# Expert weights held still in the array: gate and up products with 32-column strips of the weights stationary and 88 tokens moving

## The chip, the cores and the metric

The kernel runs on one core of a Trainium2 chip. The metric is the device time of one execution in microseconds. Three runs of the kernel before gave 1382.76, 1383.42 and 1383.52 us, so 1383.42 us is the median.

## What is computed

A trunk of two layers works on 256 frames of width 1024, all in float32. The part that the change touches is the expert layer of layer 1: a router picks two of eight experts for each frame, and each expert is a SwiGLU of inner width 3584. Cut to what matters:

```python
def moe_swiglu(h, w_router, b_router, w_gu, w_down):
    logits = (h @ w_router).astype(jnp.float32) + b_router.astype(jnp.float32)
    top_logit, top_idx = lax.top_k(logits, TOP_K)              # TOP_K = 2 of N_EXPERTS = 8
    top_w = jax.nn.softmax(top_logit, axis=-1)
    gates = jnp.sum(jax.nn.one_hot(top_idx, N_EXPERTS) * top_w[..., None], axis=-2)
    out = jnp.zeros_like(h)
    for e in range(N_EXPERTS):
        out = out + gates[..., e:e + 1] * swiglu(h, w_gu[e], w_down[e])

def swiglu(h, w_gu, w_down):
    gate, up = jnp.split(h @ w_gu, 2, axis=-1)                 # w_gu[e]: 1024 x 7168
    return (jax.nn.silu(gate) * up) @ w_down                   # w_down[e]: 3584 x 1024
```

Everything else (the mixers, the dense feed-forward block, the norms, the gated embeddings) is the same in both kernels.

## The kernel before

**Items and units.** The expert layer is worked off in items. An item is one expert with at most CAP = 96 of its tokens; with these inputs the eight experts have 53 to 84 tokens, so eight items run. An item has EU = 7 units of 512 inner features, and a unit has six granules of 1 MB of weights: four for gate and up, two for down. The granules go through a ring of six slots of 1 MB (three in the tile raw, three in the tile SC), so the transfers can be one unit ahead. SyncE's queue loads each granule as two halves of 512 KB (L318 for gate and up, L385 for down); each half waits on the count `used`, which TensorE raises when it has read the half that lay there.

**Gate and up.** For each side (gate, up) and each k of 8 slices of the inputs, `strips` multiplies three groups of 32 tokens (stationary, 32 columns of the array each) with 512 weight columns (moving). The array's 128 columns are used as four strips of 32: three strips take 384 weight columns each (L970), the fourth takes the remaining 128 weight columns of the three groups one after the other (L968). So a side and k are six matmuls, and a unit has 16 such calls. A float32 matmul of the program is two weight loads and two passes in the trace, four TensorE instructions.

**Down.** The hidden values of a unit are multiplied by the two down granules in four rounds of nine matmuls (L1005 with 512 moving columns, L1009 and L1014 with 256), with 32 tokens stationary and weights moving. They accumulate over the item's units in two banks.

**Between the two.** ScalarE takes the SiLU of the gate bank (L1425), VectorE multiplies by the up bank (L2038), and then turns the product, since the down product needs features on partitions: 16 block transposes of 32x96 (L2047) from hh into he. TensorE does the gate and up products of unit u+1 before the down product of unit u, so these steps have a whole gate and up phase of time.

**Loops.** TensorE's program is straight code for the layers before, for the first unit and for item 0; then a loop over items 1 to 6 (L1099), then the last item. Each item is straight code for one unit (gate and up of unit 1, down of unit 0) followed by an inner loop over its remaining units (L1075), whose body is one unit. The body of the inner loop has 96 + 36 = 132 matmuls, that is 528 TensorE instructions and 5 more; the body of the loop over items, which holds the straight unit, the 12 small matmuls of `turn_rows` and the inner loop once, is 1,100 instructions.

Of the kernel before, what the change touches and what calls it, by code (L numbers as in the profile page):

```python
# [22 lines left out]
ALU = mybir.AluOpType  # L23
ACT = mybir.ActivationFunctionType
# [19 lines left out]
def trunk(nc, x_d, pT_d, columns_d, norm_g, w_in_ab, a_ln_g, a_ln_b, wsT_d, w_out_ab, ffn_w_gu,  # L44
# [11 lines left out]
    ITEM = 6 * EU  # L56
    CAP = 96
    MAIN = 4 * CAP
    XTRA = T * P * 2 // (CAP + 1)
# [16 lines left out]
    with ExitStack() as ctx:  # L76
# [117 lines left out]
        xe = gain[:, 0:KT * CAP].rearrange("p (k c) -> p k c", c=CAP)  # L194
        xg_turned = xn[:, 0, 0:KT * CAP].rearrange("p (k c) -> p k c", c=CAP)
        ye = raw[:, 0, 0:D]
# [62 lines left out]
        def raw_part(g, s):  # L259
            k = raw_slot(g)  # L260
            return raw[:, k, s * HW:(s + 1) * HW] if k < RAW else more_raw[k - RAW][:, s * HW:(s + 1) * HW]

        def raw_count(g, turns):
# [45 lines left out]
        def _(sp):  # L309
# [114 lines left out]
        def _(pool):  # L424
# [69 lines left out]
            pool.wait_ge(lg_done, 1)  # L494
            pool.memset(xg_rows[0:CAP, :], 0.0).then_inc(rows_clear, 1)
            pool.wait_ge(rows_zero, 16)
# [42 lines left out]
        def _(pe):  # L539
# [416 lines left out]
            def turn_rows():  # L956

                for t in range(T):
                    for a in range(2):
                        for c in range(0, CAP, 32):  # L960
                            m = pe.matmul(PS[c:c + 32, 3, 0:2], sel16[:, t, c:c + 32], pick[:, t, a, :],
                                          start=(t == 0 and a == 0), stop=(t == T - 1 and a == 1), skip_group_check=True)
                m.then_inc(rows_psum, 1)

            def strips(bank, tokens, w, start, stop):

                for k in range(CAP // 32):
                    pe.matmul(PS[CAP:P, bank, k * P:(k + 1) * P], tokens[k], w[:, MAIN:N], start=start and k == 0, stop=stop,  # L968
                              skip_group_check=True)
# [4 lines left out]
            def landed(g, s, turns):  # L974
                pe.wait_ge(raw_full[raw_slot(g)][s], raw_count(g, turns))

            def unit_gu(g, turns, sides=(0, 1), quarters=False):

                for side in sides:
                    for k in range(KT):  # L980
                        h, j = k // HK, k % HK
                        if quarters and j % 2 == 0:
                            pe.wait_ge((xg_act, xg_ready)[j // 2], h + 1)
                        granule = g + 2 * side + h
                        if j % 2 == 0:
                            landed(granule, j // 2, turns)
                        m = strips(side, [xe[:, k, c:c + 32] for c in range(0, CAP, 32)],
                                   raw_part(granule, j // 2)[:, j % 2 * N:(j % 2 + 1) * N], k == 0, k == KT - 1)
                        if j % 2:
                            m.then_inc(used, 1)  # L990

            def turned_tokens(b, block=he):
                if b < 3:
                    return [block[:, b * P + a:b * P + a + 32] for a in range(0, CAP, 32)]
                return [block[:, k * P + CAP:(k + 1) * P] for k in range(3)]

# [3 lines left out]
            def wide_round(g, j, r, start):  # L1000
# [11 lines left out]
                def rest(k):  # L1012
                    c = k % 2 * (N // 2)
                    return pe.matmul(PS[CAP:P, 4 + k // 2, c:c + N // 2], tokens[k], w[:, N + N // 2:2 * N],  # L1014
                                     start=start and k != 1, stop=True, skip_group_check=True)
# [11 lines left out]
            def unit_down(g, n, turns, first=False):  # L1027
                pe.wait_ge(hT_ready, n)
                for j in range(2):
                    for r in range(2):  # L1030
                        landed(g + j, r, turns)
                        m = wide_round(g, j, r, first and j == 0 and r == 0)
                        m.then_inc(used, 1)

            def unit_down_last(g, n, turns, first=False):
                pe.wait_ge(hT_ready, n)
                for j in range(2):
                    for r in range(2):
                        landed(g + j, r, turns)
                        for c in range(2):  # L1040
                            m = down_round(g, j, r, c, first and j == 0 and r == 0, True)
                        m.then_inc(used, 1)

            def last_down(g, n, turns):

                pe.wait_ge(hT_ready, n)
                for j, r, c in ((0, 0, 0), (0, 0, 1), (0, 1, 0), (0, 1, 1), (1, 0, 0), (1, 1, 0), (1, 0, 1), (1, 1, 1)):
                    if c == 0:
                        landed(g + j, r, turns)
                    m = down_round(g, j, r, c, False, j == 1 and r == 1, he_last)  # L1050
# [72 lines left out]
        def _(act):  # L1123
# [292 lines left out]
            def xg(n):  # L1416

                act.wait_ge(rows_turned, n)
                for k in range(HK):
                    m = act.activation(xe[:, k, :], xg_turned[:, k, :], ACT.Copy,  # L1420
                                       scale=vcol[:, V_N12 + k:V_N12 + k + 1])
                m.then_inc(go_act, 1)

            def unit_silu():
                act.activation(sg[:, 0:MAIN], PS[:, 0, 0:MAIN], ACT.Silu).then_inc(silu_done, 1)  # L1425

# [8 lines left out]
            def output(g, turns):  # L1435

                product(g, turns)
                banks = PS[:, 4:6, :].rearrange("p b n -> p (b n)")
                act.activation(yo[0:CAP, 0:768], banks[0:CAP, 0:768], ACT.Copy)
                for k in range(3):  # L1440
                    m = act.activation(yo[32 * k:32 * (k + 1), 768:D], banks[CAP:P, 256 * k:256 * (k + 1)], ACT.Copy)
                m.then_inc(y_evac, 1)
# [43 lines left out]
            for c in range(2):  # L1486
                if c == 0:
                    act.wait_ge(y_half, Y_MOE + 1)
                else:
                    product(G_MOE, ended)  # L1490
                act.activation(ye[0:CAP, c * N:c * N + MAIN], PS[0:CAP, 4 + c, 0:MAIN], ACT.Copy).then_inc(ye_act, 1)

# [21 lines left out]
        def _(dve):  # L1514
# [501 lines left out]
            def turn_xg(n):  # L2016

                dve.wait_ge(x_rows, n * 16)
                for to in range(0, P, 32):
                    for of in range(0, CAP, 32):  # L2020
                        m = dve.transpose(xg_turned[to:to + 32, :, of:of + 32],
# [3 lines left out]
            def xg(n):  # L2025
                dve.wait_ge(rows_turned, n)
                for k in range(HK, KT):
                    m = dve.tensor_scalar(xe[:, k, :], xg_turned[:, k, :], vcol[:, V_N12 + k:V_N12 + k + 1], None,
                                          ALU.mult)
# [5 lines left out]
            def unit_hidden(n):  # L2035
                dve.wait_ge(silu_done, n)
                dve.wait_ge(hT_ready, n - 1)
                dve.tensor_tensor(hh[:, 0:MAIN], sg[:, 0:MAIN], PS[:, 1, 0:MAIN], ALU.mult).then_inc(h_ready, 1)  # L2038
# [132 lines left out]
            def last_turn(i):  # L2171

                unit_turn(i * EU + (FB + 1), (i * EU - 1) * (2 * RING) + 2 * (G_MOE + 10))

            dve.wait_ge(used, 2 * (G_MOE + 4))
            unit_hidden(FB + 1)
# [13 lines left out]
            for c in range(2):  # L2190
# [4 lines left out]
                for k in range(3):  # L2195
                    m = dve.tensor_copy(ye[32 * k:32 * (k + 1), c * N + MAIN:(c + 1) * N], PS[CAP:P, 4 + c, k * P:(k + 1) * P])
                m.then_inc(ye_rest, 1)
# [83 lines left out]
```

## Time and profile before

| | before |
|---|---|
| median of three runs | 1383.42 us |
| the profiled execution | 1383.38 us |
| its span, first to last instruction | 1381.6 us |
| outside the span | 1.8 us |
| TensorE busy | 1369.5 us (99%) |
| TensorE weight loads busy | 1180.4 us (85%) |
| VectorE busy | 675.7 us (49%) |
| ScalarE busy | 311.1 us (23%) |
| granted TensorE clock | 1.000 |

The span runs from the first to the last instruction on the chip; the time of a run is 1.8 us longer. Weight loads overlap the matmuls. Matmuls of different strips run at the same time, so the duration of one is not its share of the time: what counts is the distance of starts in one strip. The expert layer lies between about 460 and 1336 us. "issue" in a view is time in which an engine waited for nothing that the profile shows. Queue q8 of the DMA engines carries instructions, q1 the weights, q0 the gathers and scatters of token rows.

### The profile page before, as it was taken

What the parts mean: (1) busy time and instruction counts of PE and PEld (TensorE: products, weight loads), DVE (VectorE), ACT (ScalarE), POOL (GpSimd) and SP (SyncE); (2) the same over time, 40 slices, a digit from 0 to 9 for tenths busy, and PEclk for the clock granted to TensorE, in tenths of its full rate; (3) what the DMA queues carried; (4) which work ended last, traced back from release to release, by engine and by line L of the source; (5) the groups of instructions that cost most, each with busy time, mean ns of one, the idle gap of its engine ahead of it and who ended that gap; (6) DMA issues with size and microseconds to landing.
All of it is one profiled execution on the core that took longest, in us unless ns stands there. A gap on an engine that the chain in (4) does not pass through costs nothing.

```text
span 1381.6 us, 43318 instructions
## 1 busy us (share of the span) xinstructions
PE 1369.5 (99%) x18176; PEld 1180.4 (85%) x18179; DVE 675.7 (49%) x1677; ACT 311.1 (23%) x514; POOL 40.0 (3%) x61
## 2 busy tenths in 40 slices
PE   8999999999999999999999999999999999999998
PEld 6888888888788888898888888888888888889986
DVE  7886555556886533522433432532433342254454
ACT  7465444446543200100000000000000010011112
POOL 1010000000000000000000000000000000000000
PEclk9999999999999999999999999999999999999999
DMA  8477555547424999999999999999999999999970
GB/s 322 174 247 246 191 189 186 191 168 244 154 93 162 385 390 410 409 401 409 408 401 409 407 402 408 407 398 410 408 398 410 406 409 397 409 396 409 409 283 31
DMA packets 123591, 448.60 MB, mean 325 GB/s; under 512 B 14476, under 2 KB 14476, under 8 KB 122896
## 3 DMA queue, kind: packets, MB, share of 16 engines
q1 hardware_dynamic: 119232, 435.21, 82.0%
q0 software_dynamic: 4160, 12.58, 2.7%
q8 instruction: 39, 0.64, 0.2%
q14 instruction: 16, 0.13, 0.0%
q10 hardware_dynamic: 144, 0.03, 0.0%
HBM read 442.71 MB, written 7.34 MB: 326 GB/s over the span
## 4 chain that ended last, share of the span: by engine, by line
PE 98%; DVE 1%; issue 0%; ACT 0%; POOL 0%; POOLq 0%; DVEq 0%; ACTq 0%
PE PS L970 43%; PE PS L541 10%; PE PS L543 10%; PE PS L542 10%; PE PS L1005 9%; PE PS L1014 9%; PE PS L968 2%; PE PS L592 1%; PE PS L1009 1%; PE PS L836 0%; PE PS L682 0%; PE PS L610 0%; DVE he_last L2047 0%; PE PS L1103 0%; PE PS L946 0%; PE PS L926 0%
## 5 line engine op out<-in xcount | busy, mean ns | idle before, releaser
L2047 DVE STREAM_TRANSPOSE he<-junk 32x96 f32<-32x96 f32 x880 | 237.5, 270 | 212.2 <-PE PS L1005 180.4
L970 PE MATMUL PS<-raw,gain 128*32 128x384 f32 x2712 | 328.1, 491 | 0.0
L970 PE MATMUL PS<-SC,gain 128*32 128x384 f32 x2664 | 323.3, 491 | 0.0
L968 PE MATMUL PS<-raw,gain 128*32 128x128 f32 x2712 | 305.6, 273 | 0.0
L968 PE MATMUL PS<-SC,gain 128*32 128x128 f32 x2664 | 299.8, 273 | 0.0
L968 PEld LDWEIGHTS PS<-SC,gain 128*32 128x32 f32 x2664 | 290.9, 110 | 8.2
L968 PEld LDWEIGHTS PS<-raw,gain 128*32 128x32 f32 x2712 | 295.3, 110 | 0.2
L541 PE MATMUL PS<-w_hi,xT_hi 128*128 128x512 f32 x536 | 212.9, 397 | 2.8 <-DVE w_lo L1532 1.6
L543 PE MATMUL PS<-w_lo,xT_hi 128*128 128x512 f32 x536 | 209.0, 390 | 0.0
L542 PE MATMUL PS<-w_hi,xT_lo 128*128 128x512 f32 x536 | 208.7, 389 | 0.0
L1425 ACT ACTIVATE junk<-PS 128x384 f32<-128x384 f32 x56 | 27.7, 495 | 763.8 <-PE PS L970 763.8
L970 PEld LDWEIGHTS PS<-SC,gain 128*32 128x32 f32 x2664 | 190.2, 108 | 0.2
L970 PEld LDWEIGHTS PS<-raw,gain 128*32 128x32 f32 x2712 | 185.4, 108 | 0.0
L2038 DVE TENSOR_TENSOR junk<-junk,PS 128x384 f32<-128x384 f32 x56 | 31.0, 554 | 307.4 <-ACT junk L1425 297.9
L1532 DVE TENSOR_TENSOR w_lo<-raw,w_hi 128x1024 fp32r<-128x1024 f32 x144 | 168.8, 1220 | 22.1 <-ACT w_hi L1131 20.4
L1005 PE MATMUL PS<-raw,he 128*32 128x512 f32 x588 | 154.9, 593 | 0.0
L1005 PE MATMUL PS<-SC,he 128*32 128x512 f32 x588 | 154.5, 592 | 0.0
L1131 ACT ACTIVATE w_hi<-raw 128x1024 fp32r<-128x1024 f32 x144 | 145.4, 1064 | 26.9 <-PE PS L543 15.2
L1014 PE MATMUL PS<-raw,he 128*32 128x256 f32 x588 | 134.9, 379 | 0.0
L1014 PE MATMUL PS<-SC,he 128*32 128x256 f32 x588 | 134.9, 379 | 0.0
L1009 PE MATMUL PS<-raw,he 128*32 128x256 f32 x588 | 123.1, 379 | 0.0
L1009 PE MATMUL PS<-SC,he 128*32 128x256 f32 x588 | 123.1, 379 | 0.0
(312 smaller groups left out, 1512.0 us busy)
## 6 DMA issues: line engine op xcount, KB each, us to landing
raw<-in_e_w_gu SPq DMA_DIRECT2D x226, 512.0 KB, 8.5
SC<-in_e_w_gu SPq DMA_DIRECT2D x222, 512.0 KB, 8.5
SC<-in_e_w_down SPq DMA_DIRECT2D x114, 512.0 KB, 8.5
raw<-in_e_w_down SPq DMA_DIRECT2D x110, 512.0 KB, 8.5
raw<-in_ffn_w_gu SPq DMA_DIRECT2D x44, 512.0 KB, 4.7
raw<-in_w_in_c SPq DMA_DIRECT2D x32, 512.0 KB, 5.3
raw<-in_ffn_w_down SPq DMA_DIRECT2D x22, 512.0 KB, 5.3
raw<-in_w_in_ab SPq DMA_DIRECT2D x20, 512.0 KB, 6.1
```

The costliest lines, as they stand in the source:

```text
L541: pe.matmul(out, a_hi, b_hi, start=start, stop=False, skip_group_check=True)
L542: pe.matmul(out, a_lo, b_hi, start=False, stop=False, skip_group_check=True)
L543: return pe.matmul(out, a_hi, b_lo, start=False, stop=stop, skip_group_check=True)
L968: pe.matmul(PS[CAP:P, bank, k * P:(k + 1) * P], tokens[k], w[:, MAIN:N], start=start and k == 0, stop=stop, skip_group_check=True)
L970: m = pe.matmul(PS[32 * k:32 * (k + 1), bank, 0:MAIN], tokens[k], w[:, 0:MAIN], start=start, stop=stop, skip_group_check=True)
L1005: return pe.matmul(PS[32 * k:32 * (k + 1), 4, :], tokens[k], w[:, 0:N], start=start, stop=True, skip_group_check=True)
L1009: return pe.matmul(PS[32 * k:32 * (k + 1), 5, 0:N // 2], tokens[k], w[:, N:N + N // 2], start=start, stop=True, skip_group_check=True)
L1014: return pe.matmul(PS[CAP:P, 4 + k // 2, c:c + N // 2], tokens[k], w[:, N + N // 2:2 * N], start=start and k != 1, stop=True, skip_group_c ...
L1131: act.activation(w_hi[:, g % RING, part], raw_part(g, s), ACT.Copy).then_inc(hi_done, 1)
L1532: dve.tensor_tensor(w_lo[:, g % RING, part], raw_part(g, s), w_hi[:, g % RING, part].bitcast(F32), ALU.subtract).then_inc(lo_done, 1)
L2038: dve.tensor_tensor(hh[:, 0:MAIN], sg[:, 0:MAIN], PS[:, 1, 0:MAIN], ALU.mult).then_inc(h_ready, 1)
L2047: m = dve.transpose(block[to:to + 32, :].rearrange("p (b c) -> p b c", c=P)[:, :, of:of + 32], hh[of:of + 32, 0:MAIN].rearrange("p (b c) - ...
```

## The change

Four things change together, all in the expert layer.

1. **Gate and up.** `feature_strips` takes the place of `strips` there: the weights are stationary, 32 columns at a time in each of the array's four strips, and the expert's 88 tokens move. A side and k are 16 matmuls instead of 6. A strip's 32 columns are taken with a stride of two floats. The result has features on partitions and tokens along the free dimension. CAP falls from 96 to 88; the layout of the down product stays at 96 (SLOTS).
2. **Transfers.** Each granule is one transfer of 1 MB, 8 KB for each partition, that waits until both halves of its slot are read; TensorE waits once for a granule.
3. **The turn.** Since the hidden values come out with features on partitions, the 16 transposes become one copy of 128x384 from hh to he (its wait on `used`, that is until the last down product has read he, stays).
4. **The program's size.** Gate and up have 256 matmuls in a unit instead of 96, so a unit has 292 matmuls: the inner loop's body is 1,173 TensorE instructions, where it was 533, and the body of the loop over items 2,379, where it was 1,100. The whole TensorE program is 14,526 instructions, where it was 10,048. An instruction is 64 bytes.

```diff
-    CAP = 96
-    MAIN = 4 * CAP
+    CAP = 88
+    SLOTS = 96
+    MAIN = 4 * SLOTS
...
+            def load_whole(g, src, turns, first=False):
+                back, free = (RAW, lo_done) if first else (RING, used)
+                sp.wait_ge(free, turns * 2 * RING + 2 * (g - back) + 2)
+                sp.dma_start(raw_whole(g), src).then_inc(raw_full[raw_slot(g)][0], 16)
...
-                    load(g + q, src.rearrange("e g p n -> p (e g n)"), turns, first and q < RAW)
+                    load_whole(g + q, src.rearrange("e g p n -> p (e g n)"), turns, first and q < RAW)
...
-                    for s in range(2):
-                        src = dn[bass.ds(e, 1), bass.ds(u * (N * D) + (2 * j + s) * P * D, P * D)]
-                        sp.wait_ge(used, turns * 2 * RING + (2 * (g + j - RING) + s + 1))
-                        sp.dma_start(raw_part(g + j, s), src.rearrange("e (p m) -> p (e m)", p=P)).then_inc(
-                            raw_full[raw_slot(g + j)][s], 16)
+                    src = dn[bass.ds(e, 1), bass.ds(u * (N * D) + 2 * j * P * D, 2 * P * D)]
+                    load_whole(g + j, src.rearrange("e (p m) -> p (e m)", p=P), turns)
...
+            def feature_strips(side, k, w):
+
+                paired = w.rearrange("p (j c r) -> p j r c", j=2, r=2)
+                for b in range(4):
+                    for f in range(4):
+                        m = pe.matmul(PS[32 * f:32 * (f + 1), side, b * SLOTS:b * SLOTS + CAP], paired[:, b // 2, b % 2, 32 * f:32 * (f + 1)],
+                                      xe[:, k, :], start=(k == 0 and b == 0), stop=(k == KT - 1), skip_group_check=True)
+                return m
...
-                        if j % 2 == 0:
-                            landed(granule, j // 2, turns)
-                        m = strips(side, [xe[:, k, c:c + 32] for c in range(0, CAP, 32)],
-                                   raw_part(granule, j // 2)[:, j % 2 * N:(j % 2 + 1) * N], k == 0, k == KT - 1)
+                        if j == 0:
+                            landed(granule, turns)
+                        m = feature_strips(side, k, raw_part(granule, j // 2)[:, j % 2 * N:(j % 2 + 1) * N])
...
-                for to in range(0, P, 32):
-                    for of in range(0, P, 32):
-                        m = dve.transpose(block[to:to + 32, :].rearrange("p (b c) -> p b c", c=P)[:, :, of:of + 32],
-                                          hh[of:of + 32, 0:MAIN].rearrange("p (b c) -> p b c", c=P)[:, :, to:to + 32])
-                m.then_inc(hT_ready, 1)
+                dve.tensor_copy(block[:, :], hh[:, 0:MAIN]).then_inc(hT_ready, 1)
```

On TensorE, at the head of the inner loop's body (raw_full4a and 4b are the arrivals of the two halves of ring slot 4; gain holds the expert's tokens xe), before:

```order
L1075 UNCONDITIONAL_BRANCH
L1078 REGISTER_ALU [waits go_dve,go_act]
L975 ISA [waits h_ready]
L968 MATMUL PS<-SC,gain 32x128 [waits raw_full4a]
L970 MATMUL PS<-SC,gain 32x384
L968 MATMUL PS<-SC,gain 32x128 [waits raw_full4b]
L970 MATMUL PS<-SC,gain 32x384
```

There a half granule is 12 matmuls, six of each form, of which the fence shows the first two. The same place of the change:

```order
L1091 UNCONDITIONAL_BRANCH
L1094 REGISTER_ALU [waits go_dve,go_act]
L985 ISA [waits h_ready]
L992 MATMUL PS<-gain,SC 32x88 [waits raw_full4a]
L992 MATMUL PS<-gain,SC 32x88 x63
L992 MATMUL PS<-gain,SC 32x88 [waits raw_full5a]
L992 MATMUL PS<-gain,SC 32x88 x63
```

A granule is now 64 matmuls behind one wait, where it was 24 behind two. On VectorE, in the inner loop, the product with the up bank and the turn of it, before:

```order
L2037 REGISTER_ALU [waits silu_done]
L2038 TENSOR_TENSOR junk<-junk,PS 128x384 [waits hT_ready]
L2044 ISA [waits h_ready]
L2047 STREAM_TRANSPOSE he<-junk 32x3x32 [waits used]
L2047 STREAM_TRANSPOSE he<-junk 32x3x32 x15
```

and with the change (junk is the tile that hh lies in):

```order
L2053 REGISTER_ALU [waits silu_done]
L2054 TENSOR_TENSOR junk<-junk,PS 128x4x88 [waits hT_ready]
L2061 ISA [waits h_ready]
L2062 COPY he<-junk 128x384 [waits used]
```

Sixteen instructions became one behind the same waits.

## Rows read from the trace of the kernel before

**Rows 1.** The page, busy time of each engine, instruction queue, and the chain by engine
```profile
PE 1369.5 (99%) x18176; PEld 1180.4 (85%) x18179; DVE 675.7 (49%) x1677; ACT 311.1 (23%) x514; POOL 40.0 (3%) x61
...
q8 instruction: 39, 0.64, 0.2%
...
PE 98%; DVE 1%; issue 0%; ACT 0%; POOL 0%; POOLq 0%; DVEq 0%; ACTq 0%
```
**Rows 2.** Waits of SyncE's queue, 600 to 1200: line, released by, total, times, longest
```profile
SPq L318 <- PE PS L970: 197.7, 307, 1.0
SPq L385 <- PE PS L1005: 103.0, 152, 0.7
```
**Rows 3.** The chain that ended last, 610 to 650: start, us, what
```profile
612.98 10.26 PE PS L970 x94
...
628.64 10.26 PE PS L970 x94
644.30 5.79 PE PS L970 x53
```
**Rows 4.** Windows: length, PE, PEld, DVE, ACT, POOL busy (x), clock, DMA, GB/s
```profile
628.16:643.82 15.66, 15.66 (x271) 13.47 (x265) 4.88 (x17) 0.50 (x1) 0.00 (x0) 1.00 1.03 409
683.55:793.44 109.89, 109.89 (x1867) 95.43 (x1862) 41.27 (x143) 6.46 (x15) 1.90 (x2) 1.00 1.03 406
460.00:1336.00 876.00, 875.77 (x14959) 773.39 (x14958) 345.92 (x1185) 66.24 (x136) 16.51 (x18) 1.00 1.02 405
448.00:452.00 4.00, 3.87 (x24) 2.32 (x23) 2.23 (x4) 1.98 (x5) 0.84 (x2) 1.00 1.02 424
```
**Rows 5.** Timeline of PE, 628.6 to 629.9: start, us, instruction
```profile
628.69 0.27 PE L968 MATMUL PS<-SC,gain 128*32 128x128 f32 x1
...
628.80 0.27 PE L968 MATMUL PS<-SC,gain 128*32 128x128 f32 x1
```
**Rows 6.** Groups of PE, PEld and DVE, 600 to 1200: busy, mean ns | idle
```profile
L968 PE MATMUL PS<-SC,gain 128*32 128x128 f32 x1847 | 208.0, 273 | 0.0
L1005 PE MATMUL PS<-SC,he 128*32 128x512 f32 x456 | 119.9, 592 | 0.0
L1014 PE MATMUL PS<-SC,he 128*32 128x256 f32 x456 | 104.6, 379 | 0.0
L968 PEld LDWEIGHTS PS<-SC,gain 128*32 128x32 f32 x1844 | 201.4, 110 | 6.5
L2047 DVE STREAM_TRANSPOSE he<-junk 32x96 f32<-32x96 f32 x615 | 166.0, 270 | 149.9 <-PE PS L1005 142.3
```
**Rows 7.** Timeline of PE, around 365 and 371
```profile
365.27 1.30 PE L815 MATMUL PS<-SC 128*32 128x32 f32 x128
...
370.83 0.77 PE L836 MATMUL PS<-SC 128*32 128x16 f32 x69
372.77 0.69 PE L836 MATMUL PS<-SC 128*32 128x16 f32 x59 [1.17 <-issue]
```
**Rows 8.** Windows of straight-line code, columns as in Rows 4
```profile
366.10:371.65 5.55, 5.50 (x143) 4.33 (x129) 4.79 (x5) 2.08 (x3) 0.00 (x0) 1.00 0.79 286
381.90:386.10 4.20, 4.20 (x141) 3.33 (x140) 4.08 (x3) 0.00 (x0) 0.00 (x0) 1.00 0.01 4
...
1251.60:1258.54 6.94, 6.94 (x135) 6.94 (x130) 1.84 (x6) 2.38 (x3) 1.00 (x2) 1.00 1.02 407
1258.54:1265.17 6.63, 6.63 (x128) 6.63 (x123) 5.39 (x14) 0.00 (x0) 0.00 (x0) 1.00 1.02 407
```
**Rows 9.** Transfers, 610 to 1243: the queues that had any, packets, MB, share
```profile
q1 hardware_dynamic: 69737, 253.93, 101.3%
q0 software_dynamic: 1120, 2.61, 1.3%
q14 instruction: 2, 0.02, 0.0%
```
**Rows 10.** Transfers, 366 to 370.3, 370.3 to 372.8, 373.7 to 375.2: packets, queues
```profile
DMA packets 383, 1.41 MB, mean 327 GB/s; under 512 B 40, under 2 KB 40, under 8 KB 383
...
q1 hardware_dynamic: 383, 1.41, 91.1%
...
DMA packets 68, 0.23 MB, mean 90 GB/s; under 512 B 16, under 2 KB 16, under 8 KB 67
...
q8 instruction: 1, 0.02, 2.4%
...
DMA  0090000000000000000000000000000000000000
...
q8 instruction: 1, 0.02, 5.4%
```

More of the change, by code:

```diff
@@ L194, in trunk @@
         xe = gain[:, 0:KT * CAP].rearrange("p (k c) -> p k c", c=CAP)
-        xg_turned = xn[:, 0, 0:KT * CAP].rearrange("p (k c) -> p k c", c=CAP)
+        hid_cols = hh[:, 0:MAIN].rearrange("p (b c) -> p b c", c=SLOTS)
+        gate_out, up_out = (PS[:, side, 0:MAIN].rearrange("p (b c) -> p b c", c=SLOTS)[:, :, 0:CAP] for side in range(2))
+        xg_turned = xn[:, 0, 0:KT * SLOTS].rearrange("p (k c) -> p k c", c=SLOTS)
         ye = raw[:, 0, 0:D]
@@ L261, in raw_part, with raw_whole @@
             return raw[:, k, s * HW:(s + 1) * HW] if k < RAW else more_raw[k - RAW][:, s * HW:(s + 1) * HW]
+        def raw_whole(g):
+            k = raw_slot(g)
+            return raw[:, k, :] if k < RAW else more_raw[k - RAW]
         def raw_count(g, turns):
@@ L494, in _ @@
             pool.wait_ge(lg_done, 1)
-            pool.memset(xg_rows[0:CAP, :], 0.0).then_inc(rows_clear, 1)
+            pool.memset(xg_rows[0:SLOTS, :], 0.0).then_inc(rows_clear, 1)
             pool.wait_ge(rows_zero, 16)
@@ L960, in turn_rows @@
                         for c in range(0, CAP, 32):
-                            m = pe.matmul(PS[c:c + 32, 3, 0:2], sel16[:, t, c:c + 32], pick[:, t, a, :],
+                            end = min(c + 32, CAP)
+                            m = pe.matmul(PS[c:end, 3, 0:2], sel16[:, t, c:end], pick[:, t, a, :],
                                           start=(t == 0 and a == 0), stop=(t == T - 1 and a == 1), skip_group_check=True)
@@ L965, in strips @@
             def strips(bank, tokens, w, start, stop):
-                for k in range(CAP // 32):
-                    pe.matmul(PS[CAP:P, bank, k * P:(k + 1) * P], tokens[k], w[:, MAIN:N], start=start and k == 0, stop=stop,
+                for k in range(SLOTS // 32):
+                    pe.matmul(PS[SLOTS:P, bank, k * P:(k + 1) * P], tokens[k], w[:, MAIN:N], start=start and k == 0, stop=stop,
                               skip_group_check=True)
@@ L972, in strips, with landed @@
                 return m
-            def landed(g, s, turns):
-                pe.wait_ge(raw_full[raw_slot(g)][s], raw_count(g, turns))
+            def landed(g, turns):
+                pe.wait_ge(raw_full[raw_slot(g)][0], raw_count(g, turns))
+            def feature_strips(side, k, w):
[5 more added lines that the diff above has]
+                return m
             def unit_gu(g, turns, sides=(0, 1), quarters=False):
@@ L992, in turned_tokens @@
             def turned_tokens(b, block=he):
-                if b < 3:
-                    return [block[:, b * P + a:b * P + a + 32] for a in range(0, CAP, 32)]
-                return [block[:, k * P + CAP:(k + 1) * P] for k in range(3)]
+                return [block[:, b * SLOTS + a:b * SLOTS + a + 32] for a in range(0, SLOTS, 32)]
             def down_round(g, j, r, c, start, stop, block=he):
@@ L1029, in unit_down @@
                 for j in range(2):
+                    landed(g + j, turns)
                     for r in range(2):
-                        landed(g + j, r, turns)
                         m = wide_round(g, j, r, first and j == 0 and r == 0)
@@ L1037, in unit_down_last @@
                 for j in range(2):
+                    landed(g + j, turns)
                     for r in range(2):
-                        landed(g + j, r, turns)
                         for c in range(2):
@@ L1047, in last_down @@
                 for j, r, c in ((0, 0, 0), (0, 0, 1), (0, 1, 0), (0, 1, 1), (1, 0, 0), (1, 1, 0), (1, 0, 1), (1, 1, 1)):
-                    if c == 0:
-                        landed(g + j, r, turns)
+                    if r == 0 and c == 0:
+                        landed(g + j, turns)
                     m = down_round(g, j, r, c, False, j == 1 and r == 1, he_last)
@@ L1419, in xg @@
                 for k in range(HK):
-                    m = act.activation(xe[:, k, :], xg_turned[:, k, :], ACT.Copy,
+                    m = act.activation(xe[:, k, :], xg_turned[:, k, 0:CAP], ACT.Copy,
                                        scale=vcol[:, V_N12 + k:V_N12 + k + 1])
@@ L1438, in output @@
                 banks = PS[:, 4:6, :].rearrange("p b n -> p (b n)")
-                act.activation(yo[0:CAP, 0:768], banks[0:CAP, 0:768], ACT.Copy)
+                act.activation(yo[0:SLOTS, 0:768], banks[0:SLOTS, 0:768], ACT.Copy)
                 for k in range(3):
-                    m = act.activation(yo[32 * k:32 * (k + 1), 768:D], banks[CAP:P, 256 * k:256 * (k + 1)], ACT.Copy)
+                    m = act.activation(yo[32 * k:32 * (k + 1), 768:D], banks[SLOTS:P, 256 * k:256 * (k + 1)], ACT.Copy)
                 m.then_inc(y_evac, 1)
@@ L2019, in turn_xg @@
                 for to in range(0, P, 32):
-                    for of in range(0, CAP, 32):
+                    for of in range(0, SLOTS, 32):
                         m = dve.transpose(xg_turned[to:to + 32, :, of:of + 32],
@@ L2037, in unit_hidden @@
                 dve.wait_ge(hT_ready, n - 1)
-                dve.tensor_tensor(hh[:, 0:MAIN], sg[:, 0:MAIN], PS[:, 1, 0:MAIN], ALU.mult).then_inc(h_ready, 1)
+                dve.tensor_tensor(hid_cols[:, :, 0:CAP], sg[:, 0:MAIN].rearrange("p (b c) -> p b c", c=SLOTS)[:, :, 0:CAP], up_out,
+                                  ALU.mult).then_inc(h_ready, 1)
             def unit_turn(n, finished=None, block=he):
@@ L2173, in last_turn @@
                 unit_turn(i * EU + (FB + 1), (i * EU - 1) * (2 * RING) + 2 * (G_MOE + 10))
+            step(dve.memset(hid_cols[:, :, CAP:SLOTS], 0.0))
             dve.wait_ge(used, 2 * (G_MOE + 4))
```

10 lines of the change are left out of this document (5 added, 5 removed).

## The prediction, before the result was known

> **What bounds the kernel now.** I read the page first: TensorE is busy for 99% of the span and makes up 98% of the chain that ended last [rows 1]. The reader is to see that nothing else counts unless it makes TensorE wait. Then the waits of SyncE's queue: its loads of gate and up, and of down, wait for TensorE to release a slot, some 300 us of waiting in 600 us [rows 2]. So TensorE holds the ring, but with little to spare: the longest wait is 1.0 us, and the windows show the queues moving 409 GB/s with a share of 1.03 [rows 4]. The chain gives the beat: pieces of 10.26 us of gate and up start at 612.98, 628.64 and 644.30, so a unit takes 15.66 us [rows 3], and an item 109.89 us [rows 4], which is seven units and 0.27 us.
>
> **Gate and up without any wait.** The first passes of L968 start 0.109 us apart in the fourth strip [rows 5] (their 273 ns [rows 6] hold the way through the array). A call has six in that strip, 0.654 us; 16 calls are 10.46 us, and the other 5.2 us of the unit are the down product. In the change a call is 32 weight loads and 32 passes, eight of each in a strip. From 512 to 256 moving columns a pass goes from 592 to 379 ns [rows 6], 0.83 ns a column, so 88 columns take 109 - 40 x 0.83 = 76 ns, and a call 8 x 76 = 0.606 us. That is 0.049 us less a call, 0.78 us less a unit: 14.88 us.
>
> Are the weight loads hidden at that pace? They show 110 ns each [rows 6], but 128 loads and 128 passes of 32 columns went through in 1.30 us [rows 7]: 32 pairs a strip, 41 ns each, under 76. In all that is 10 ns a pair, and the change needs one in 19 ns. So the work itself fits: I take the gain whole, 56 units x 0.78 = 44 us, if nothing else binds. Strided weight columns do not occur before; the bounds are nothing and a load four times as long, 164 ns a pair, 16 calls x 8 x (164 - 76) ns = 11.3 us a unit, 630 us. I take nothing, since the loads have 35 ns to spare in each pair.
>
> One rule speaks against this. The 10 ns a pair of the row stand for both passes and loads [rows 7]. The Trainium skill, TensorE: Matmul & The Clock Gate, section Back-to-back issue gap, states that starts of matmuls never lie closer than about 25 ns. By it a call would take 32 x 25 = 0.8 us, and 896 calls 174 us more than at 0.606; the trace disagrees, with 128 passes in 1.30 us. I go by the row.
>
> **Transfers.** Rows of 4 KB move 409 GB/s; where the loads of 8 KB rows ran, 448 to 452, the window shows 424 [rows 4]. A unit has 6.29 MB: 15.4 us at 409, 14.84 at 424. Bounds: no faster than now, or 424. I take 424; then transfers (with gathered rows some 105.5 us an item) would bind just above TensorE. It matters only if TensorE is not slowed otherwise. Whole granules ask TensorE to wait for all of a megabyte, and give a slot back one half later, some 1.2 us; five slots are then ahead, 12 us of transfers, which hide it. Without that cover it would be 1.2 us a granule.
>
> **VectorE.** Sixteen transposes of 270 ns become one copy: VectorE's 4.9 us of a unit [rows 4] fall towards 1. Nobody waits for it: the turn of a unit has the gate and up phase of the next, 10 us, as its cover (it would cost its 4.3 us each unit otherwise). It gains nothing.
>
> **Instructions.** This decides. TensorE's code comes as 39 packets of q8, 0.64 MB [rows 1], 16 KB or 256 instructions each. Straight code shows it: 265 and 251 records lie between packets at 1251.60, 1258.54 and 1265.17 [rows 8]. What has run stays, up to a size: from 610 to 1243, where the loop over items turns, no instruction packet of q8 arrives [rows 9]; that loop is 1,100 instructions, 4.3 blocks. The program before never runs a larger loop, so the trace does not show whether 2,379 instructions (9.3 blocks) stay. It shows what a late block costs. In the stretch of short matmuls at 371 TensorE stands still from 371.60 to 372.77 for "issue", in the middle of 128 equal passes [rows 7]. 272 records back from there is 366.1 [rows 8], about one block; no packet came in 366 to 370.3, with the transfers at 327 GB/s, one came in 370.3 to 372.8, and the next in the second slice after 373.7 [rows 10], 1.0 us after work resumed. So the fetch of a block begins when the one before it begins to run, one block ahead, and was ready about 6.6 us later there. With the queues idle the start is 1.0 us after the boundary instead of 4.2, so about 3.4 us; two blocks of some 280 records in 4.20 us at 381.9 [rows 8] did not stall. In the loaded expert layer blocks of 6.63 us did not stall either. So the time of a fetch, call it L, lies between 3.4 and 6.6 us.
>
> Gate and up now use 64 instructions in 0.606 us: a block of 256 in 2.42 us, where it was 6.6 to 7.5. Every block that is not held thus costs L - 2.42. The unit loop, 4.6 blocks, is about as large as the loop that stayed before, and I take it to stay. The loop over items I take to go out, since it is more than twice the largest that is seen to stay. The row shows no more than this. The Trainium skill, Runtime: NRT & Kernel Launch, section Instruction fetch mechanics, gives TensorE room for 2048 instructions in blocks of 256 and calls the prefetch sequential, with a stall at a taken branch out of the window; by it 2,379 do not fit, and the sum would be the one below.
>
> An item then fetches ten blocks: the first on the way back, with all of L seen; two behind down products of 5.2 us, hidden; seven at L - 2.42. L is nearer to which end? While TensorE stalls, a megabyte is used in L instead of 2.42 us, and its transfer takes 2.5 us, so the queues are busy little more than half the time. I take 4.5 us, a little under the middle. Then
>
> - an item: 7 x 14.88 + 0.27 = 104.4 us, plus 4.5 + 7 x 2.08 = 19.1, is 123.5 us, 13.6 more than 109.9; six turns of the loop: +81 us
> - code that runs straight once (first unit, item 0, last item; 20 blocks of gate and up, three hidden): 17 x 2.08 = +35 us, less 14 faster units, 11 us: +24 us
>
> The sum is 1383.4 + 81 + 24 = 1489 us, made against the profiled execution, 1383.38 us, which stands 0.04 us below the median. At L = 3.4 the same sum gives 1418, at 6.6 it gives 1626; a microsecond of L is 65 us.
>
> **The rivals.**
>
> *It goes faster: code is never late, or stays.* For it: before, the loop stays without a packet [rows 9], and how much more would stay isn't seen. If code costs nothing, transfers at 424 GB/s bind at 105.5 us an item, 4.4 less: 8 items, -35 us, 1348 us. If the item loop stays but the straight code is late once, about 25 us come back: 1360 to 1380. It decides at L below 2.4 us or at room for ten blocks. Against it: the hole at 371.60.
>
> *Part of the loop stays.* If half of the seven boundaries are held, an item saves 7 to 9 us, and the sum is about 1440 at 4.5 us and 1400 at 3.4.
>
> *Even the unit loop goes out.* It touches up to six blocks and has one more on its way. Then each of 56 units pays L + 3 x (L - 2.42), about 10 us: 1383 - 44 + 560 = 1900 us. Against it: the 4.3 blocks before stayed.
>
> *The pairs are slower than 76 ns,* by stride, by loads that don't hide, or by that floor of 25 ns: at 100 ns a pair in a strip 896 x 8 x 24 ns = +172 us, on top of or in place of the stalls, 1510 to 1660 us. Against it: 41 ns a pair at 365.27 [rows 7].
>
> *The transfers don't gain* from 8 KB rows: alone it would leave 1383, no change; beside the stalls it adds nothing.
>
> **How the numbers follow.** The stalls with the loop going out: 0.64, 1489 us, own range 1418 to 1580. Part of it stays: 0.09. Code costs nothing, 1348: 0.08; item loop stays, 1360 to 1380: 0.08. Unit loop out: 0.06. Slow pairs: 0.04. No change: 0.01. The range from 1362 to 1580 leaves out the 1348, the 1900 and half of the slow pairs and the longest fetches, 0.2 together. A measurement of this kernel tells about 0.2%, 2.8 us, from no change. Faster holds both cases of code that stays, 0.16; same 0.02; slower 0.82.
>
> **What would show it.** Right: q8 packets all through 610 to 1243, about ten an item in place of none; gaps of TensorE for "issue" of some 2 us at every fourth call of gate and up in the first two units of an item, and a longer one at the item's start; later units of an item at about 14.9 us without gaps; the queues' share under 0.95; about 100 q8 packets in all (57 of the program once, ten more for each turn after the first) against 39; SyncE waiting longer for L992. Steps wrong: passes of L992 more than 76 ns apart in a strip without gaps (pace of pairs); TensorE waiting for DMA (transfers); gaps in every unit (the unit loop). The prediction is wrong altogether if the loop over items shows no q8 packet, or if blocks come within 2.4 us.

## The result: 1509 us, 9% slower

The change takes 1509.21 us, the median of four runs (1505.07 to 1513.84), against 1383.22 us in the same job (1382.76 to 1383.52): the ratio is 1.0908, 95% interval 1.0891 to 1.0926. Forecast was 1489 us. The profiled execution has a span of 1507.0 us, 125.4 us more than before.

The page of the change: busy time, the queue that carries instructions, the chain by engine, and the groups that answer to [rows 6].

```profile
PE 1376.0 (91%) x36099; PEld 1236.1 (82%) x36099; DVE 450.7 (30%) x838; ACT 309.6 (21%) x514; POOL 41.4 (3%) x61
...
q8 instruction: 116, 1.90, 0.5%
...
PE 91%; issue 8%; DVE 1%; ACT 0%; POOL 0%; POOLq 0%; DVEq 0%; ACTq 0%
...
L992 PE MATMUL PS<-gain,SC 128*32 128x88 f32 x14208 | 309.5, 244 | 61.4 <-issue 61.4
...
L2062 DVE COPY he<-junk 128x384 f32<-128x384 f32 x55 | 19.8, 361 | 219.5 <-PE PS L1021 195.6
```

Beside [rows 1] the reader sees a new weight in the chain, "issue" with 8% where it had 0%, and 116 instruction packets instead of 39. TensorE's waits between 600 and 1300 name nothing else; SyncE's queue waits longer for TensorE than in [rows 2] (12.2 us where it was 1.0), so the ring is full and the queues stand idle meanwhile:

```profile
PE PS L992 <- issue: 86.7, 33, 4.8
PE PS L971 <- issue: 3.3, 4, 1.7
PE PS L1030 <- issue: 3.0, 4, 1.4
```

```profile
SPq L383 <- PE PS L992: 385.1, 152, 12.2
SPq L383 <- PE PS L1021: 157.1, 76, 4.2
```

Where [rows 9] has no packet of q8 while the loop over items turns, the change has 68 between 610 and 1340:

```profile
q1 hardware_dynamic: 34783, 253.30, 87.3%
q0 software_dynamic: 1728, 3.12, 1.5%
q8 instruction: 68, 1.11, 0.6%
```

One turn of the loop over items in the chain, from the last unit of one item (706.89) to the second turn of the inner loop in the next (775.33). L992 is gate and up, L1021 and L1030 the down product, L971 the small products that pick rows:

```profile
706.89 9.70 PE PS L992 x508
...
721.84 4.78 issue
726.62 0.51 PE PS L992 x4
727.12 3.24 issue
730.37 6.22 PE PS L992 x248
736.69 1.06 issue
...
740.35 3.40 issue
743.75 3.97 PE PS L992 x128
...
756.70 1.36 issue
758.06 2.63 PE PS L992 x128
760.69 2.35 issue
763.04 5.87 PE PS L992 x211
...
772.29 0.54 issue
...
775.33 9.80 PE PS L992 x501
```

The stalls lie in the straight unit and in the first turn of the inner loop, and nowhere else in an item; the later turns of the inner loop have none. The seven pieces of issue add up to 16.7 us. But there is a second loss in the same rows: 128 passes of a granule take 3.97 us at 743.75, where a granule is 2.42 us at full pace. The windows show why (columns as in [rows 4]; the third number from the end is the granted clock, 1.00 for 2.4 GHz and 0.50 for 1.2 GHz):

```profile
552.31:567.20 14.89, 14.89 (x596) 14.34 (x591) 0.88 (x2) 0.47 (x1) 0.00 (x0) 1.00 1.01 423
...
730.37:732.00 1.63, 1.63 (x47) 1.63 (x50) 0.00 (x0) 0.00 (x0) 0.00 (x0) 0.50 0.05 10
732.00:734.00 2.00, 2.00 (x91) 2.00 (x84) 0.00 (x0) 0.00 (x0) 0.00 (x0) 0.77 0.00 0
734.00:735.50 1.50, 1.50 (x85) 1.44 (x79) 0.00 (x0) 0.00 (x0) 0.00 (x0) 1.00 0.24 38
...
743.75:746.00 2.25, 2.25 (x64) 2.25 (x67) 0.00 (x0) 0.00 (x0) 0.00 (x0) 0.50 0.31 69
...
763.04:766.50 3.46, 3.46 (x112) 3.46 (x116) 0.00 (x0) 0.00 (x0) 0.00 (x0) 0.59 0.41 163
...
736.42:1244.20 507.78, 443.91 (x16414) 414.62 (x16406) 52.87 (x152) 24.88 (x60) 8.35 (x8) 0.94 0.89 352
```

A unit without stalls takes 14.89 us. After TensorE stood still for most of 8.5 us its granted clock was 0.50 when it began again, and it came back to 1.00 some 3 us later; after the stall of 3.40 us the same. After the stall of 2.35 us it was low for some 3 us too, though another stall of that length, at 1141.09, was not followed by a lower clock. At 0.50 passes start 36 to 38 ns apart instead of 19. The last row holds four items: 126.9 us each, of which TensorE was busy 111.0 and idle 16.0. Seven units at 14.89 us and the 0.27 us of an item would be 104.5 us busy, so 6.5 us an item are lost while TensorE counts as busy. The lower clock is most of that: by the granted clock of the trace 9.0 us of an item's busy time lie at 0.50, where half of it, 4.5 us, would do at 1.00. For the rest, the last passes before a stall run out with none behind them: 128 passes between two stalls take 2.63 us at full clock (758.06) instead of 2.42, 1.5 us for seven stalls.

### The profile page after: what moved, and what is told of

Read it like the earlier page. It is cut to its first block, busy times and chain, and to the rows that moved or that the text cites. A ratio compares the mean times of both kernels' runs of the same rounds, so it can differ in the third digit from the quotient of the medians.

```text
span 1507.0 us, 76989 instructions
## 1 busy us (share of the span) xinstructions
PE 1376.0 (91%) x36099; PEld 1236.1 (82%) x36099; DVE 450.7 (30%) x838; ACT 309.6 (21%) x514; POOL 41.4 (3%) x61
## 4 chain that ended last, share of the span: by engine, by line
PE 91%; issue 8%; DVE 1%; ACT 0%; POOL 0%; POOLq 0%; DVEq 0%; ACTq 0%
PE PS L992 39%; PE PS L550 9%; PE PS L552 9%; PE PS L551 9%; PE PS L1021 9%; PE PS L1030 5%; PE PS L1025 3%; PE PS L980 2%; PE PS L601 1%; PE PS L845 0%; PE PS L691 0%; PE PS L978 0%; PE PS L619 0%; PE PS L1119 0%; PE PS L955 0%
## 5 line engine op out<-in xcount | busy, mean ns | idle before, releaser
L992 PE MATMUL PS<-gain,SC 128*32 128x88 f32 x14208 | 309.5, 244 | 61.4 <-issue 61.4
L992 PEld LDWEIGHTS PS<-gain,SC 128*32 128x32 f32 x14208 | 305.5, 113 | 72.3 <-issue 69.9
L992 PE MATMUL PS<-gain,raw 128*32 128x88 f32 x14464 | 318.2, 248 | 50.6 <-issue 50.4
L992 PEld LDWEIGHTS PS<-gain,raw 128*32 128x32 f32 x14464 | 304.7, 115 | 55.7 <-issue 55.5
L1441 ACT ACTIVATE junk<-PS 128x352 f32<-128x352 f32 x56 | 26.0, 464 | 886.8 <-PE PS L992 886.8
L2054 DVE TENSOR_TENSOR junk<-junk,PS 128x352 f32<-128x352 f32 x56 | 29.2, 521 | 563.9 <-ACT junk L1441 548.4
L1021 PE MATMUL PS<-SC,he 128*32 128x512 f32 x588 | 147.8, 592 | 0.0
L1021 PE MATMUL PS<-raw,he 128*32 128x512 f32 x588 | 144.4, 595 | 0.0
L1030 PE MATMUL PS<-SC,he 128*32 128x256 f32 x588 | 135.8, 379 | 3.0 <-issue 3.0
L1030 PE MATMUL PS<-raw,he 128*32 128x256 f32 x588 | 135.4, 380 | 0.0
L550 PEld LDWEIGHTS PS<-w_hi,xT_hi 128*128 128x128 f32 x536 | 100.8, 188 | 22.8 <-issue 2.8
L552 PEld LDWEIGHTS PS<-w_lo,xT_hi 128*128 128x128 f32 x536 | 100.6, 188 | 21.5
L551 PEld LDWEIGHTS PS<-w_hi,xT_lo 128*128 128x128 f32 x536 | 100.8, 188 | 19.9 <-issue 0.2
L1030 PEld LDWEIGHTS PS<-SC,he 128*32 128x32 f32 x588 | 64.2, 110 | 24.1 <-issue 7.1
```

The lines of the kernel that those rows point to most:

```text
L550: pe.matmul(out, a_hi, b_hi, start=start, stop=False, skip_group_check=True)
L551: pe.matmul(out, a_lo, b_hi, start=False, stop=False, skip_group_check=True)
L552: return pe.matmul(out, a_hi, b_lo, start=False, stop=stop, skip_group_check=True)
L992: m = pe.matmul(PS[32 * f:32 * (f + 1), side, b * SLOTS:b * SLOTS + CAP], paired[:, b // 2, b % 2, 32 * f:32 * (f + 1)], xe[:, k, :], star ...
L1021: return pe.matmul(PS[32 * k:32 * (k + 1), 4, :], tokens[k], w[:, 0:N], start=start, stop=True, skip_group_check=True)
L1030: return pe.matmul(PS[SLOTS:P, 4 + k // 2, c:c + N // 2], tokens[k], w[:, N + N // 2:2 * N], start=start and k != 1, stop=True, skip_group ...
```

## The experiments

Two theories stood against each other: that TensorE's code arrives late, since the loop over items no longer stays in the engine's store and gate and up run through a block in 2.42 us; and that the new form is slow by itself, by its weight loads, its pairs or its transfers. Kernels that mix the row order of whole granules with that of half granules (e1_whole, e2_halves, e3h_wide64_halves and e10_halves_late) pair the hidden features with other rows of the down weights, so their output isn't the reference's; the work is the same.

**Whole granules alone** (e1_whole). The kernel before with the change's transfers and waits, `strips` and transposes kept:

```diff
-                    load(g + q, src.rearrange("e g p n -> p (e g n)"), turns, first and q < RAW)
+                    load_whole(g + q, src.rearrange("e g p n -> p (e g n)"), turns, first and q < RAW)
...
-                        if j % 2 == 0:
-                            landed(granule, j // 2, turns)
+                        if j == 0:
+                            landed(granule, turns)
...
```

> The kernel before with whole granules of 1 MB alone (one transfer, one wait for each); products, transposes and TensorE's program stay. The theory (late TensorE code makes the loss, transfers have no part in it): TensorE keeps its 15.66 us a unit, 1383 us, within 3 us of before. Rival (waiting for a whole megabyte costs the time): the loss is here, towards 1500 us. If the transfers were what held the kernel before, it would fall by up to 20 us.

Measured: 1383.21 us, ratio 0.9996 (0.9987 to 1.0006). Neither the wait for a megabyte nor the larger rows move the time where TensorE binds.

**Half granules in the change** (e2_halves), the reverse:

```diff
-                    load_whole(g + q, src.rearrange("e g p n -> p (e g n)"), turns, first and q < RAW)
+                    load(g + q, src.rearrange("e g p n -> p (e g n)"), turns, first and q < RAW)
...
```

> The change with the half granules of before (512 KB each, two waits). Theory of late code: the queues idle while TensorE stands still and run a full ring ahead afterwards, so half granules cost nothing: 1509 us, within 8. Rival (the megabyte transfers or their wait make the loss): well under 1480 us.

Measured: 1543.52 us, ratio 1.1164 (1.1145 to 1.1184). Both expectations missed: half granules cost another 34 us. An item of it in the windows:

```profile
740.08:871.42 131.34, 111.33 (x4112) 103.16 (x4105) 13.21 (x38) 6.21 (x15) 2.09 (x2) 0.94 0.92 342
```

TensorE is busy as long as in the change; the idle time is 20.0 us where it was 16.0. From the chain's piece at 649.26 to that at 1307.82 five turns of the loop take 131.7 us each, where the change has 126.9: six turns make 29 of the 31 us that lie between the two profiled executions. So the transfers change how late the code is. After the stalls of over 0.5 us between 610 and 1300 the next instruction packet starts 1.97 us after TensorE resumes, in the median, where the change has 1.39; from a packet's start to the resumption both have 2.4 us.

**Both halves issued late** (e10_halves_late). Half granules again, but each half waits until the whole slot is read:

```diff
-                        sp.wait_ge(free, turns * 2 * RING + (2 * (g - back) + s + 1))
+                        sp.wait_ge(free, turns * 2 * RING + (2 * (g - back) + (s + 1 if g < G_MOE else 2)))
...
```

> The change with half granules whose two transfers both wait until the whole slot is read, so that they are issued when the change issues its whole granule; packets of 4 KB as with half granules. Half granules cost 34 us more than whole ones in the change. If that is the smaller packets (an instruction packet waits behind more of them): about 1543 us again. If it is the earlier issue (more transfers waiting when code is fetched): about 1509 us.

Measured: 1548.35 us, ratio 1.1188 (1.115 to 1.1226). The earlier issue isn't it; what is left of the two is the smaller packets. That an instruction packet waits behind more of them fits the later start (1.85 us in the median here), but the queue itself was not seen, and the smaller packets were not tested apart from there being twice as many transfers.

**64 columns held still** (e3_wide64).

```diff
-                    for f in range(4):
-                        m = pe.matmul(PS[32 * f:32 * (f + 1), side, b * SLOTS:b * SLOTS + CAP], paired[:, b // 2, b % 2, 32 * f:32 * (f + 1)],
+                    for f in range(2):
+                        m = pe.matmul(PS[64 * f:64 * (f + 1), side, b * SLOTS:b * SLOTS + CAP], paired[:, b // 2, b % 2, 64 * f:64 * (f + 1)],
```

> The change with 64 weight columns held still instead of 32: two strips, 8 matmuls a call instead of 16, 164 in a unit instead of 292, and a loop over items of about 1,355 TensorE instructions (5.3 blocks). A strip still has eight passes of 88 columns a call, so the work's time is the same if the weight loads hide. Theory of late code: the loop stays, no q8 packet inside it, item 105 to 106 us, 1345 to 1360 us. Rival (weights held still are slow in themselves, by stride or by pairs): still over 1450 us, with passes further apart than 76 ns in a strip and no gaps for issue.

Measured: 1367.46 us, ratio 0.9881 (0.9865 to 0.9898), the fastest kernel here, 16 us under before and 142 under the change. Four items of it in the windows:

```profile
697.81:1124.49 426.68, 426.68 (x9235) 356.82 (x9234) 52.86 (x152) 24.85 (x60) 8.34 (x8) 1.00 1.01 415
```

106.67 us an item, TensorE busy throughout at full clock; and between 700 and 1230 the queues list no instruction packet:

```profile
q1 hardware_dynamic: 29843, 217.30, 99.6%
q0 software_dynamic: 1440, 2.61, 1.7%
```

The same strided weights held still, the same 88 tokens and the same transfers are fast once the loop stays. It lies 7 us above the range that was expected: gate and up of a unit take 9.89 us in the chain instead of 9.70, a unit 15.19, and the straight code still has a few stalls of 1 to 2 us.

**64 columns with half granules** (e3h_wide64_halves), both edits above together.

> 64 columns held still everywhere, with half granules instead of whole ones. With 64 columns and whole granules an item takes 106.67 us at a share of the queues near 1. Theory (there the transfers bind, and half granules move 409 instead of 424 GB/s): items of 108.5 to 109 us, 1380 to 1388 us. Rival (TensorE's unit of 15.19 us binds, the form of the transfers does nothing): 1367 us.

Measured: 1385.37 us, ratio 1.0008 (0.9999 to 1.0018). An item takes 109.87 us at 404 GB/s, and TensorE waits for transfers:

```profile
PE PS L1033 <- DMA SC<-in_e_w_down: 5.7, 5, 2.1
```

So with late code out of the way 8 KB rows are worth 18 us, as a bound by transfers.

**One loop, 32 columns** (e4_one_loop). The products of the change, but items 1 to 6 run all seven units in the inner loop; ScalarE sets the down banks to zero after reading them:

```diff
             with pe.Fori(1, last_item) as i:
-                item(i, False)
+                pe.wait_ge(sel_ready, i + 3)
+                turn_rows()
+                with pe.Fori(0, EU) as u:
...
+                    unit_gu(G_MOE + 4, i * EU + u)
+                    pe.wait_ge(y_evac, i + 1)
+                    unit_down(G_MOE + 8, i * EU + u + (FB + 1), i * EU + u)
...
```

> The change with 32 columns as it is, but in items 1 to 6 the first unit is run by the inner loop too (seven turns): ScalarE sets the down banks to zero after it has read them, so that no first product is needed, and the small products that pick rows come ahead of the loop. The loop over items is then about 1,220 TensorE instructions (4.8 blocks) instead of 2,379, with the same products. Theory of late code: no q8 packet from item 2 on, item 105 to 107 us instead of 128, 6 x 22 less: 1370 us, 1362 to 1380; granted clock 1.0 in the loop. Rival (the form or the waits are slow): 1500 us or more.

Measured: 1403.69 us, ratio 1.015 (1.0126 to 1.0174), 106 us under the change with the same matmuls in the loop. Four items:

```profile
713.95:1139.73 425.78, 421.57 (x16405) 380.22 (x16400) 52.49 (x152) 29.18 (x68) 8.36 (x8) 1.00 1.01 416
```

106.4 us each, clock 1.00; and between 700 and 1230 the queues are full and list no instruction packet:

```profile
q1 hardware_dynamic: 29889, 217.64, 99.8%
q0 software_dynamic: 1440, 2.61, 1.6%
```

This is the test of the cause: the same products at the same pace, in a smaller loop. What else differs (ScalarE's zeroing, TensorE's wait for it, the rows picked ahead of the inner loop) takes no work away. The time stays 24 us over the expected range's top, since the straight code before the loop and the loop's first turn were late here as well: TensorE is busy for 114.82 of the 130.00 us of that first stretch,

```profile
470.69:600.69 130.00, 114.82 (x4378) 107.00 (x4373) 21.31 (x81) 7.76 (x18) 2.19 (x2) 0.98 0.89 346
```

and I had put all of the gain on six items, where the first turn still fetches.

**Where the size decides** (e5_unroll2, e6_unroll3). The kernel before with the inner loop of items 1 to 6 written out two or three times:

```diff
-                with pe.Fori(1, EU - 1 if last else EU) as u:
+                times = 1 if last or first else 3
+                with pe.Fori(0, 5 if last else 6 // times) as v:
+                    for j in range(times):
+                        u = v * times + (j + 1)
...
```

> The kernel before with the inner loop of items 1 to 6 written out twice (three turns of two units): the same instructions run, but the loop over items is about 1,633 TensorE instructions, 6.4 blocks, where it was 1,100. If loops of up to eight blocks stay: no q8 packet in the loop and 1383 us, within 3. If only some five blocks stay: as the next kernel.

> The kernel before with the inner loop of items 1 to 6 written out three times: the loop over items is about 2,166 instructions, 8.5 blocks, with the slow pace of before (a block in 6.6 us or more). Theory: it no longer stays, some nine q8 packets an item; blocks fetched ahead are in time at that pace, so only the way back costs, one block on demand and what of the next is late, 5 to 8 us an item as in the change: 1413 to 1431 us. Rival (size does not matter, only that weights are held still): no packets and 1383 us.

Measured: 1384.18 us, ratio 1.0001 (0.9991 to 1.0011) for two; 1416.32 us, ratio 1.0232 (1.0215 to 1.0249) for three. Queues between 700 and 1230 with three, and its waits of TensorE:

```profile
q1 hardware_dynamic: 54978, 200.21, 96.6%
...
q8 instruction: 48, 0.79, 0.6%
```

```profile
PE PS L968 <- issue: 21.4, 5, 4.6
```

With two no q8 packet comes in that stretch. With three the loop is fetched each time, and there is one stall of up to 4.6 us an item, on the way back; in between, where a block takes 6.6 us or more, there is none. The kernel before can be made slow by nothing but a longer loop.

**64 columns in the straight unit only** (e7_straight64).

```diff
-                    unit_gu(G_MOE + 4, i * EU, (0,))
+                    unit_gu(G_MOE + 4, i * EU, (0,), n=32 if last else 64)
...
```

> The change with 64 columns held still only in the straight unit of items 1 to 6, 32 columns everywhere else: the loop over items is about 1,867 instructions, 7.3 blocks, with 32-column code in most of it. If eight blocks stay: no packets in the loop, items of about 106.5 us, and the straight code outside the loop as late as in the change: 1385 to 1400 us. If it doesn't stay: the inner loop's first turn is late as before and the way back costs 5 us or more: 1440 to 1470 us.

Measured: 1499.84 us, ratio 1.0828 (1.0806 to 1.085). Neither number came: 1,867 instructions do not stay either, 41 packets between 700 and 1230, and an item is 126 us. In the chain the straight unit has no stall behind its first two, but the first turn of the inner loop has:

```profile
718.07 4.84 issue
722.91 0.56 PE PS L992 x4
723.47 3.31 issue
726.77 6.97 PE PS L992 x124
...
747.75 3.85 issue
...
758.56 3.56 issue
```

Two of them are longer than the 2 us that I had put on a late block. In the trace the packet that ends the second starts at 759.96, 4.0 us after the block before it began at 755.93, where the change's median is 1.39; from its start to the resumption are 2.2 us, near the 2.45 of the change. Why it starts so late is not shown.

**A slow pace in a loop that doesn't stay** (e9_wide64_unroll3): e3_wide64 with `times = 3` as above.

> 64 columns held still everywhere, and the inner loop of items 1 to 6 written out three times: a loop over items of about 2,670 instructions, 10.4 blocks, larger than that of the change, that goes through a block of gate and up in 4.9 us instead of 2.42. Theory (what costs is the pace: a block fetched ahead is there some 4 us after its request): no stalls inside, only the way back as in the long loop of the kernel before, 6 to 8 us an item: 1403 to 1420 us. Rival (any code that does not stay costs as in the change): items of 125 us, 1475 us or more.

Measured: 1474.71 us, ratio 1.066 (1.0633 to 1.0687), near the rival's figure, but the chain doesn't show the rival's stalls:

```profile
824.31 5.44 issue
829.75 0.56 PE PS L992 x4
830.31 2.15 issue
...
857.11 0.28 issue
...
874.84 0.96 issue
...
897.73 4.88 issue
...
906.10 0.59 issue
```

12.5 of the 14.3 us lie on two ways back: that of the loop over items (824.31 and 830.31) and that of the inner loop at 897.73, which I had overlooked: three units written out are about 1,980 instructions and don't stay either. Inside, at 4.9 us a block, stalls are 0.28 to 0.96 us in this item, where none were expected. So the pace matters, if not as fully as expected, and the way back is dear whatever the pace. The busy time of an item grows as well, to 112.4 of 126.4 us from 106.67.

**128 columns held still** (e8_wide128).

```diff
-                    for f in range(4):
+                    for f in range(1):
+                        m = pe.matmul(PS[:, side, b * SLOTS:b * SLOTS + CAP], paired[:, b // 2, b % 2, :],
```

> 128 columns held still (4 matmuls a call, 100 in a unit): the smallest code, all of it stays. Theory, from the passes of 96 columns with 128 held still in the trace before, 112 ns apart: a weight load of 128 columns does not hide behind 88 moving columns, a call takes 8 x 112 = 0.9 us, a unit 19.6 us: about 1600 us, without gaps for issue. If the load hides: 76 ns, and about 1365 us.

Measured in one run: 1658.27 us. Gate and up of a unit are one piece like this, 128 passes 119 ns apart, without a stall; 112 ns were expected:

```profile
703.40 15.27 PE PS L992 x128
```

In a strip of 32 or 64 columns they are 76 and 77 ns apart (9.70 and 9.89 us for 128). So 88 moving columns hide a load of 32 or 64 columns, as far as distances tell, and not one of 128.

## Why the prediction was right, and which terms were off

- **The pace of gate and up** was right: 14.88 us a unit forecast, 14.89 measured. The stride cost nothing, and 512 passes in 9.70 us, 19 ns apart, bear out [rows 7]. The Trainium skill, TensorE: Matmul & The Clock Gate, section Back-to-back issue gap, has about 25 ns as the least distance; passes that go to four strips come closer than that here.
- **Transfers** moved 423 GB/s where TensorE took them in time, as taken, and were not the bound, as the sum had it. That their form adds nothing beside the stalls was wrong: half granules cost 34 us through the fetches (e2_halves, e10_halves_late).
- **VectorE** fell from 675.7 to 450.7 us busy and gave nothing, as forecast.
- **The unit loop stays, the loop over items doesn't**: right. e4_one_loop and e3_wide64 show that this is the cause. Twelve packets an item came, ten were forecast. The Trainium skill, Runtime: NRT & Kernel Launch, section Instruction fetch mechanics, gives TensorE room for 2048 instructions; the trace agrees that 2,379 do not stay, but 1,867 did not either (e7_straight64).
- **The stalls of an item**: 19.1 us forecast with L = 4.5, 16.0 measured. From resuming to the next packet's start are 1.39 us in the median and from there to the next resumption 2.45, an L of 3.8 us; the value taken was too high. The first block was right (4.78 us against 4.5), but only a few instructions of it are used, so that a second long stall of 3.24 us follows at once: the way back cost 8.0 us where 4.5 stood, and the late blocks 8.7 in the turn shown where seven at 2.08 stood, 14.6. (One reading behind L is off by a place: the mark in [rows 10] is in the third slice after 373.7, not the second; the 1.0 us is right.)
- **The clock** was the main term that was missing: about 4.5 of the 6.5 us an item by which the busy time grew; the passes that run out before each stall are most of the rest. The sum kept TensorE at full clock, as it was all through the kernel before.
- **The sum.** The chain's piece of 9.80 us comes at 647.24 and five turns later at 1281.81: 126.9 us an item against 109.89 [rows 4], 17.0 more where 13.6 stood. Six turns are 102 us against 81; the rest of the 125.4 us is 23 against 24 for the straight code. The 3.1 us too much for the stalls and the 6.5 us that were missing cancel in part and leave 3.4 us an item; that the forecast is only 20 us off owes something to this luck. So does the straight code, whose stalls hold the lower clock too (0.94 in the mean between 462 and 552).

The rivals: loop or code that stays (1348, 1360 to 1380) did not happen, but e3_wide64 at 1367 us is just that case made true. That part of the loop stays is excluded by twelve packets an item for a loop of 9.3 blocks; why it is twelve was not taken apart. Slow pairs and a unit loop that goes out are excluded by the windows of a unit, 14.89 us all busy.

## What to carry to other kernels

Count the instructions of a loop body before cutting a product into smaller ones: here a loop of 1,633 TensorE instructions ran without fetching, one of 1,867 did not, and each way back into a loop that doesn't stay cost 4 to 9 us of standing still; where between the two the bound lies was not measured. Inside, the pace decides: in the change blocks of 256 instructions in 2.42 us stalled for up to 3.4 us, in e9_wide64_unroll3 blocks in 4.9 us for up to 1.2, and in e6_unroll3 blocks in 6.6 us or more not at all. When a faster form makes code late, make it coarser first (64 columns instead of 32: 9.89 us for a unit's gate and up instead of 9.70, with half the instructions); and reckon with a half clock behind stalls of a few microseconds.

## What was not expected of the hardware

- After two or three stalls of an item, those of the way back and that of 3.40 us among them, TensorE worked at a granted clock of 0.50 for some 3 us: about 4.5 us an item beside 16.0 of standing still.
- Instruction packets came later beside another form of the data transfers: with 4 KB instead of 8 KB rows they started 1.97 us after TensorE resumed instead of 1.39, and the idle time of an item rose from 16.0 to 20.0 us, with TensorE's work unchanged.
- 64 weight columns held still have passes of 88 columns nearly as close as 32 (9.89 us for a unit's gate and up against 9.70), while 128 columns need 15.27 us.
